# The order of TensorE's work in the last round of a mixture of experts: both halves of the down products ahead of the spread

## The chip, the cores and the metric

The kernel runs on one core of one Trainium2 chip. The metric is the device time of one launch in microseconds (us), the median over runs. TensorE (PE in the profile) multiplies, VectorE (DVE) and ScalarE (ACT) move and transform what it leaves in PSUM, GpSimd (POOL) fetches rows by index, SyncE (SP) issues the loads of the weights.

## The reference

One inference step of a two-layer decoder for 256 prompt tokens and 8 sample tokens (264 columns in the kernel), model width 1024. The first layer mixes tokens by retention, the second by gated linear attention (GLA); behind each mixer stands a mixture of 64 experts, of which each token takes 8. Cut to what matters here:

```
for i in range(2):
    h = modulate(x, norm_mix_g[i], sh1, sc1)
    x = x + g1 * mixer_i(h)                      # i = 0: retention, i = 1: GLA
    h = modulate(x, norm_ffn_g[i], sh2, sc2)     # RMS norm, scale, shift
    x = x + g2 * moe_ffn(h)
return rmsnorm(x, final_norm_g), states
# an expert on its rows: (silu(x @ w_gate) * (x @ w_up)) @ w_down,
#     w_gate, w_up: 1024 x 256, w_down: 256 x 1024, all float32, 1 MB each
# routed = sum over a token's 8 experts of weight * expert(row), and a shared expert is added
```

## The kernel before, in words

`experts(k, layer)` is called once for each layer. It goes through the 64 experts in 16 rounds of 4 (`ROUNDS`, `EPI`); rounds 13 to 15 are light ones, with 32 rows for each of the four experts, so that one tile of 128 rows holds the four. `LAST` is round 15. The weights pass through a ring of 12 slots of 1 MB: four gates, four ups, four downs of a round, issued by SP in that order (L2319 to L2359). In the last round the four down matrices come in two column halves: first the four first halves (semaphore `s_first_half`), then the four second halves (the slots' own semaphores, which `wait_light(pe, LAST, "moe_w_down")` waits for).

A light round on TensorE (`pe_round`, L2529): the gate products (`four_up`, L2449), then the spread of the round before (`spread`, L2510), which adds its rows to their tokens by a one-hot product for each of the 8 chunks of 128 model columns, then the up products (`four_up` again), two transposes of the hidden rows (`hidden_first`, L2526), a copy of them by ScalarE (L3016), and the down products (`four_down`, L2459): half 0 writes PSUM bank 6, half 1 bank 7, each 16 instructions over 512 columns. In the last round `pe_round` ends with half 0.

`last_spread` (L2481) follows. TensorE takes its instructions in order. It waits for ScalarE's copy of half 0 (`s_part`, L3038), multiplies chunks 0 to 3 (L2495, float32, two instructions each), then waits for the second halves of the down matrices and multiplies half 1, then chunks 4 to 7. Each chunk has PSUM bank 0 or 1 by turns, so that a chunk waits for VectorE's add of the chunk two before it (`s_add`; `add_last`, L2868 to L2873, three instructions, into x). `follow(pe, c)` is one step of what comes next and needs that add of chunk c: in layer 0 the sum of the squares of x over the chunk for the next norm (`nxt.sum`, L549, which waits for ScalarE's square, L532), in layer 1 three transposes of x for the output (`x_rows`, L1960). Before the change follow 0 and 1 stand behind half 1, and follow c - 2 behind each chunk c from 4 on; the caller (`tail_tensor`) issues follow 6 and 7.

ScalarE in the last round copies half 0 (L3038), then runs `beside_copies`: a small Sqrt that loads a table (L3403), and in layer 0 the squares of chunks 0 to 3; then it copies half 1, and in layer 0 squares chunks 4 to 7.

Behind layer 0's last sum come TensorE's conditioning products (L484), VectorE's norm (L566 to L575), ScalarE's shift (L543, eight chunks of h), and the first projection of GLA (L1403), which needs h and the first weights `in_gla_w_in`. Behind layer 1's last transposes come the output norm and the stores.

`keep_clock(k, bank, n)` (L470) issues n products of the identity with itself, 128x128 in float32, into a PSUM bank that nobody reads; one product is two instructions.

Of the kernel before, what the change touches and what calls it, by code (L numbers as in the profile page):

```python
# [21 lines left out]
P = 128  # L22
D = 1024
DC = D // P
TP = 256
NS = 8
T = TP + NS
# [35 lines left out]
LIGHT_BLOCKS = [(e, 32 * e) for e in range(EPI)]  # L63
# [217 lines left out]
LIGHT_PLACE = {ne: i for i, ne in enumerate(LIGHT_ROUND)}  # L281
# [5 lines left out]
def slot(k, n, inner):  # L287

    s = n % RING
    return k.ring[:, s * SLOT:(s + 1) * SLOT].rearrange("p (k n) -> p k n", n=inner)  # L290
# [179 lines left out]
def keep_clock(k, bank, products):  # L470

    for _ in range(products):
        k.nc.tensor.matmul(k.ps[:, bank, 0:P], k.ident, k.ident, start=True, stop=True)
# [22 lines left out]
def next_rows(k):  # L496

    return k.rstd[:, T:T + 256]
# [19 lines left out]
class Norm:  # L518
# [27 lines left out]
    def sum(self, pe, c):  # L546

        pe.wait_ge(self.s_sq, c + 1)
        mm = self.k.nc.tensor.matmul(self.sums_at, self.k.ones, self.sq[:, c, :], start=(c == 0), stop=(c == DC - 1))  # L549
        if c == DC - 1:  # L550
            mm.then_inc(self.s_sum, 1)
# [1494 lines left out]
def experts(k, layer):  # L2046

    nc, inp = k.nc, k.inp
# [14 lines left out]
    LAST = ROUNDS - 1  # L2063
    RANKED = NE - EPI

    def tiles(r):
        if not isinstance(r, int) or r < HEAVY:
            return PAIRS
        return PAIRS + 1 if r == HEAVY else 1

    def light(r):
        return tiles(r) == 1

    def done_tiles(r, late):
        return sum(tiles(q) for q in range(r)) if isinstance(r, int) else PAIRS * r + late
# [14 lines left out]
    last_token = slot_area[:, 0:T]  # L2090
# [19 lines left out]
    last_rows = row_area[:, 0:D]  # L2110
# [116 lines left out]
    def hidden_chunk(p, m):  # L2227
        return hid[:, p, :].rearrange("p (q m) -> p m q", m=FC)[:, m, :]

    def place(kind, e, of=PLACE):  # L2230
        return n_moe + of[(kind, e)]
# [222 lines left out]
    def four_down(p, blocks, half, of=PLACE):  # L2454

        for m in range(FC):
            for e, lo in blocks:
                n = place("moe_w_down", e, of)
                mm = nc.tensor.matmul(k.ps[lo:lo + 32, 6 + half, :], hid_t[:, p, m, lo:lo + 32],  # L2459
                                      slot(k, n, D)[:, m, half * 512:(half + 1) * 512],  # L2460
                                      start=(m == 0), stop=(m == FC - 1))
                if m == FC - 1 and half == 1 and blocks is HEAVY_BLOCKS and e == len(HEAVY_TILE) - 1:
                    mm.then_inc(h_done, 1)
                elif m == FC - 1 and half == 1 and (e, lo + 32) not in blocks:
                    mm.then_inc(k.ring_free[n % RING], 1)
        if half == 0:
            mm.then_inc(s_dn, 1)

    def wait_light(pe, r, name):

        for e in range(EPI):
            n = place(name, e, LIGHT_PLACE)
            pe.wait_ge(k.ring_full[n % RING], 16 * (r + n // RING + 1))
# [7 lines left out]
    def last_spread(pe, follow):  # L2481

        d = done_tiles(LAST, 0)
        pe.wait_ge(s_htc, LAST + 1)
        for half in range(2):
            if half:
                wait_light(pe, LAST, "moe_w_down")
                four_down(0, LIGHT_BLOCKS, 1, LIGHT_PLACE)
                if follow:
                    follow(pe, 0)  # L2490
                    follow(pe, 1)
            pe.wait_ge(s_part, 2 * d + 1 + half)
            for c in range(4 * half, 4 * half + 4):
                pe.wait_ge(s_add, DC * (LAST + 1) + c - 1)
                nc.tensor.matmul(k.ps[:, c % 2, 0:T], last_rows[:, c * P:(c + 1) * P], last_token,  # L2495
                                 start=True, stop=True).then_inc(s_scat, 1)
                if half and follow:
                    follow(pe, c - 2)

    def spread(pe, r, late=0, n=PAIRS):  # L2500

# [20 lines left out]
    def hidden_first(pe, p, bank, d, at=0):  # L2522

        pe.wait_ge(s_hid, d + p + 1)
        for m in range(FC):
            mm = nc.tensor.transpose(k.ps[:, bank, at + m * P:at + (m + 1) * P], hidden_chunk(p, m), ident)  # L2526
        mm.then_inc(s_hidt, 1)

    def pe_round(pe, r, late=0):  # L2529
        first, last = isinstance(r, int) and r == 0, isinstance(r, int) and r == LAST  # L2530
        heavy = tiles(r) > PAIRS
        d = done_tiles(r, late)
# [6 lines left out]
        for p in range(0 if light(r) or heavy else PAIRS):  # L2539
# [3 lines left out]
            for j, name in enumerate(("moe_w_gate", "moe_w_up")):  # L2543
# [3 lines left out]
                for c in range(DC):  # L2547
                    for e in (2 * p, 2 * p + 1):
                        n, lo = place(name, e), CAP * (e % 2)
                        w = slot(k, n, DE)  # L2550
                        if first and (name, e) in ROUND[0:EARLY]:
# [3 lines left out]
                                              start=(c == 0), stop=(c == DC - 1))  # L2555
                        if c == DC - 1:
                            mm.then_inc(k.ring_free[n % RING], 1)
        for j, name in enumerate(("moe_w_gate", "moe_w_up") if heavy else ()):
            for p in range(PAIRS):
# [3 lines left out]
                for c in range(DC):  # L2563
                    for e in (2 * p, 2 * p + 1):
# [3 lines left out]
                                              start=(c == 0), stop=(c == DC - 1))  # L2568
# [12 lines left out]
        for p in range(min(tiles(r), PAIRS)):  # L2581
            if heavy:
                hidden_first(pe, p, 6, d, at=p * DE)
            else:
                hidden_first(pe, p, 6 + p, d)
        if not last:
            if not first:
                pe.wait_ge(s_add, DC * r + DC)
            if not heavy:
                gather(pe, r + 1, late)  # L2590
            pe.wait_ge(s_htc, r + 1)
            if heavy:
                four_slots_first(pe, r).then_inc(h_done, 1)
            elif isinstance(r, int) and light(r + 1):
                four_slots_first(pe, r + 1).then_inc(s_ht, 1)
            else:
                slots_first(pe)
# [797 lines left out]
    def squares_of(act, chunks):  # L3395

        for c in chunks:
            act.wait_ge(s_add, DC * (LAST + 1) + c + 1)
            nxt.square(act, c)

    def beside_copies(act):

        nc.scalar.activation(silu[0:1, 0, 0:1], ident[0:1, 0:1], ACT.Sqrt)  # L3403
        if layer == 0:
            squares_of(act, range(DC // 2))

    def tail_scalar(act):

        rounds_scalar(act)
        act.wait_ge(s_cleared, 1)  # L3410
        pairs = extra_pairs["act"]
        here, more, usual, done = branch(act, "act", pairs, twice=True)
        with nc.body(more, valid_engines=here):
            scalar_round(act, LAST)
            with act.Fori(0, pairs) as i:
                for b in range(2):
                    act.wait_ge(x_gat, 2 * i + b + 1)
                    nc.scalar.copy(xg[:, 0, 4 * b:4 * b + 4, :].rearrange("p c n -> p (c n)"), k.ps[:, b, :])\
                        .then_inc(x_got, 1)
                act.wait_ge(x_own, i + 1)  # L3420
                act.wait_ge(x_scat, DC * i + DC)
                nc.scalar.copy(slot_token[:, 0, 0:TP].rearrange("p (t n) -> p t n", t=2),
                               k.ps[:, 4, 0:2 * EW].rearrange("p (t n) -> p t n", t=2)[:, :, 0:P])
                nc.scalar.copy(slot_token[:, 0, TP:T], k.ps[:, 4, TT * EW - 6 - NS:TT * EW - 6])\
                    .then_inc(x_tok, 1)
                act.wait_ge(x_gu, i + 1)
                nc.scalar.activation(silu[:, 0, :], k.ps[:, 2, 0:DE], ACT.Silu).then_inc(x_sil, 1)
                act.wait_ge(x_hidt, i + 1)
                nc.scalar.copy(hid_t[:, 0].rearrange("p m s -> p (m s)"), k.ps[:, 3, 0:DE]).then_inc(x_hidtc, 1)
                for half in range(2):  # L3430
                    act.wait_ge(x_dn, 2 * i + half + 1)
                    nc.scalar.copy(row_parts[:, 0, 0, half * 512:(half + 1) * 512], k.ps[:, 6 + half, :])\
                        .then_inc(x_hi, 1)
            nc.scalar.activation(silu[0:1, 0, 0:1], ident[0:1, 0:1], ACT.Sqrt)
            if layer == 0:
                act.wait_ge(x_add, pairs * DC + DC)
                for c in range(DC):
                    nxt.square(act, c)
            act.br(done)
        with nc.body(usual, valid_engines=here):  # L3440
            scalar_round(act, LAST, beside=beside_copies)
            if layer == 0:
                squares_of(act, range(DC // 2, DC))
            act.br(done)
        nc.switch_bb(done)
        if layer == 0:
            nxt.scalar(act)
            wait_used(k, act, next_group[-1])
            nc.scalar.copy(next_rows(k), k.ps[:, 4, 0:256]).then_inc(tail.s_rows, 1)
        else:  # L3450
            act.wait_ge(s_final, 1)
            final_squares(k, 0, sums, junk).then_inc(tail.s_sums, 1)
            act.wait_ge(s_final, 2)
            nc.scalar.activation(small, k.x[:, :, TP:T], ACT.Square).then_inc(s_final, 1)
            final_squares(k, 1, sums, junk).then_inc(tail.s_sums, 1)
# [34 lines left out]
```

## Time and profile before

| what | us |
|---|---|
| median of 3 runs | 1581.24 |
| lowest and highest | 1580.17, 1581.70 |
| the profiled execution, its own time | 1583.97 |
| the profiled execution, its span | 1582.1 |
| PE busy | 1492.0 |
| DVE busy | 701.7 |
| ACT busy | 358.4 |
| mean rate of the loads and stores | 367 GB/s |

### The profile page before, as it was taken

The page shows a single profiled execution, that of the slowest core. Times are in us where ns is not written, and L with a number is a line of the kernel's source. Part 1 is how long each engine was busy: PE and PEld are TensorE (multiplying, and loading weights), DVE is VectorE, ACT ScalarE, POOL GpSimd, SP SyncE. Part 2 cuts the span into 40 slices and gives each one's busy share as a digit, 9 for nine tenths or more (in the row PEclk, how much of TensorE's full clock was granted, in tenths as well). Part 3 has the DMA queues.
Part 4 walks back from the last instruction along what each step waited for, and adds up shares of the span by engine and source line. Part 5 has one row for each costly group of instructions (what it writes and reads, how often), then busy time and mean ns, then how long its engine had stood idle before and what let it go on. Part 6 is the DMA issues. An engine that isn't in the chain of part 4 may idle for free. (4 is left out here: it accounts for less than half of the span.)

```text
span 1582.1 us, 29469 instructions
## 1 busy us (share of the span) xinstructions
PE 1492.0 (94%) x11156; PEld 983.7 (62%) x11156; DVE 701.7 (44%) x1998; ACT 358.4 (23%) x760; POOL 92.0 (6%) x117
## 2 busy tenths in 40 slices
PE   6999999999999999999996899999999999999966
PEld 4778765687665566566553587776566566565533
DVE  3204535315465545534354335443745544543543
ACT  3012443203212111111120255432112211211111
POOL 0000100001000100000000000001000000010000
PEclk9999999999999999999998999999999999999988
DMA  9997699429999999999999983999999999999996
GB/s 363 389 369 270 252 399 399 184 101 370 392 412 420 420 420 420 421 418 419 413 384 415 358 280 120 347 364 335 416 419 421 420 420 420 420 419 414 391 407 247
DMA packets 153295, 580.27 MB, mean 367 GB/s; under 512 B 16893, under 2 KB 62113, under 8 KB 104938
## 3 DMA queue, kind: packets, MB, share of 16 engines
q1 hardware_dynamic: 137642, 535.74, 85.7%
q0 software_dynamic: 14912, 40.91, 6.7%
q10 hardware_dynamic: 640, 2.26, 0.4%
q8 instruction: 64, 1.05, 0.3%
q14 instruction: 37, 0.30, 0.1%
HBM read 566.12 MB, written 26.90 MB: 375 GB/s over the span
## 5 line engine op out<-in xcount | busy, mean ns | idle before, releaser
L2553 PE MATMUL ps<-ring,scratch 128*64 128x256 f32 x3008 | 330.7, 380 | 1.9 <-DMA ring<-in_moe_w_up 1.9
L2553 PEld LDWEIGHTS ps<-ring,scratch 128*64 128x64 f32 x3008 | 215.5, 137 | 107.2 <-issue 3.6
L2612 PE MATMUL ps<-ring,scratch 128*64 128x512 f32 x816 | 186.8, 598 | 1.2 <-DVE scratch L2970 0.9
L722 PE MATMUL ps<-hT,ring 128*128 128x264 f32 x768 | 179.4, 387 | 0.0
L2510 PE MATMUL ps<-scratch 128*128 128x264 bf16 x1344 | 165.9, 276 | 3.7 <-DVE xT L2873 2.0
L722 PEld LDWEIGHTS ps<-hT,ring 128*128 128x128 f32 x768 | 145.4, 191 | 28.9 <-issue 2.5
L2898 DVE SCALAR_TENSOR_TENSOR scratch<-scratch,ps 128x256 f32<-128x256 f32 x60 | 28.8, 481 | 302.2 <-ACT scratch L3007 280.2
L2510 PEld LDWEIGHTS ps<-scratch 128*128 128x128 bf16 x1344 | 116.7, 97 | 53.8 <-issue 15.4
L2865 DVE TENSOR_TENSOR scratch<-scratch,ps 128x264 f32<-128x264 f32 x224 | 95.3, 429 | 65.0 <-PE ps L2510 64.9
L2612 PEld LDWEIGHTS ps<-ring,scratch 128*64 128x64 f32 x816 | 53.3, 136 | 107.1 <-issue 75.1
L3007 ACT ACTIVATE scratch<-ps 128x256 f32<-128x256 f32 x60 | 23.1, 384 | 392.9 <-PE ps L2553 320.3
L2257 POOL DMA_INDIRECT scratch<-h_rows,scratch x58 | 57.7, 996 | 868.6 <-DVE scratch L2251 820.0
L3042 ACT CAST scratch<-ps 128x512 bf16<-128x512 f32 x112 | 65.5, 587 | 142.5 <-PE ps L2612 126.0
L2970 DVE TENSOR_TENSOR scratch<-ps,scratch 128x512 f32<-128x512 f32 x112 | 76.8, 686 | 34.5 <-ACT scratch L3042 34.5
L1403 PE MATMUL ps<-hT,ring 128*128 128x264 f32 x384 | 88.9, 386 | 1.9 <-DMA ring<-in_gla_w_in 1.9
L1403 PEld LDWEIGHTS ps<-hT,ring 128*128 128x128 f32 x384 | 72.0, 190 | 15.0 <-DMA ring<-in_gla_w_in 2.4
L2958 DVE TENSOR_TENSOR scratch<-scratch 128x512 bf16<-128x512 f32 x112 | 77.5, 692 | 3.9
L2416 PE MATMUL ps<-tab,scratch 128*128 128x128 f32 x464 | 62.8, 278 | 11.7 <-DVE scratch L2773 9.0
L2449 PE MATMUL ps<-ring,scratch 128*32 128x256 f32 x768 | 51.0, 424 | 19.5 <-DMA ring<-in_moe_w_gate 11.2
L2416 PEld LDWEIGHTS ps<-tab,scratch 128*128 128x128 f32 x464 | 50.2, 141 | 23.8 <-DVE scratch L2773 15.2
L2773 DVE COPY scratch<-ps 128x512 f32<-128x512 f32 x58 | 40.1, 692 | 56.0 <-PE ps L2416 56.0
L982 DVE SCALAR_TENSOR_TENSOR ring<-ring,rstd 128x512 f32<-128x512 f32 x64 | 41.3, 688 | 49.2 <-ACT rstd L1135 26.1
(413 smaller groups left out, 1542.3 us busy)
## 6 DMA issues: line engine op xcount, KB each, us to landing
ring<-in_moe_w_up SPq DMA_DIRECT2D x128, 1024.0 KB, 18.7
ring<-in_moe_w_gate SPq DMA_DIRECT2D x124, 1024.0 KB, 18.3
ring<-in_moe_w_down SPq DMA_DIRECT2D x118, 1024.0 KB, 15.9
ring<-in_ada_w SPq DMA_DIRECT2D x48, 1024.0 KB, 12.4
ring<-in_ret_w_in SPq DMA_DIRECT2D x24, 1024.0 KB, 16.8
ring<-in_state_ret SPq DMA_DIRECT2D x16, 1024.0 KB, 14.2
out_ret_sample<-ring POOLq DMA_DIRECT2D x16, 1024.0 KB, 8.9
ring<-in_gla_w_in SPq DMA_DIRECT2D x12, 1024.0 KB, 11.8
```

The lines of the kernel that those rows point to most:

```text
L722: mm = nc.tensor.matmul(k.ps[:, bank, 0:T], w[:, c, m * P:(m + 1) * P], k.h[:, c, :], start=(c == 0), stop=(c == DC - 1))
L1403: mm = nc.tensor.matmul(k.ps[:, bank, 0:T], w[:, c, m * P:(m + 1) * P], k.h[:, c, :], start=(c == 0), stop=(c == DC - 1))
L2257: pool.indirect_dma_start(xtok_of(p), None, h_rows[:, :], bass.IndirectOffsetOnAxis(ap=rows[:, p:p + 1], axis=0), bounds_check=ABSENT - 1, ...
L2416: mm = nc.tensor.transpose(k.ps[:, b, c * P:(c + 1) * P], xtok_of(p)[:, d0:d0 + P], ident)
L2449: mm = nc.tensor.matmul(k.ps[lo:lo + 32, bank, j * DE:(j + 1) * DE], xg_of(p)[:, c, lo:lo + 32], slot(k, n, DE)[:, c, :], start=(c == 0), ...
L2510: mm = nc.tensor.matmul(k.ps[:, c % 2, 0:T], parts_of(p)[:, s, c * P:(c + 1) * P], slot_token[:, p, :], start=(p == 0 and s == 0), stop=(p ...
L2553: mm = nc.tensor.matmul(k.ps[lo:lo + CAP, 2 + p, j * DE:(j + 1) * DE], xg[:, p, c, lo:lo + CAP], w[:, c, :], start=(c == 0), stop=(c == DC ...
L2612: mm = nc.tensor.matmul(k.ps[lo:lo + CAP, 6 + half, :], hid_t[:, p, m, lo:lo + CAP], w[:, m, half * 512:(half + 1) * 512], start=(m == 0), ...
L2865: nc.vector.tensor_tensor(acc[:, c, :], acc[:, c, :], k.ps[:, c % 2, 0:T], ALU.add).then_inc(s_add, 1)
L2958: nc.vector.tensor_tensor(parts_of(p)[:, 2, cols], rest[:, half], parts_of(p)[:, 1, cols], ALU.subtract).then_inc(s_part, 1)
L2970: nc.vector.tensor_tensor(rest[:, half], k.ps[:, 6 + half, :], parts_of(p)[:, 0, cols], ALU.subtract).then_inc(s_rest, 1)
L3042: nc.scalar.copy(parts_of(p)[:, 0, cols], k.ps[:, 6 + half, :]).then_inc(s_rhi, 1)
```

## The change

`last_spread` now runs half 1 of the down products directly behind half 0 (behind the wait for its weights), and only then all eight chunks of the spread; from chunk 2 on each chunk c is followed by follow c - 2. The waits of a chunk stay. In the second layer's last round, three `keep_clock` products stand ahead of the transposes of the hidden rows and six behind them, into bank 7. ScalarE no longer squares chunks 0 to 3 between its two copies in layer 0; it squares all eight behind the second copy.

```diff
     def last_spread(pe, follow):
 
         d = done_tiles(LAST, 0)
+
+        def second_half():
+            wait_light(pe, LAST, "moe_w_down")
+            four_down(0, LIGHT_BLOCKS, 1, LIGHT_PLACE)
+
+        def chunk(c):
+            pe.wait_ge(s_add, DC * (LAST + 1) + c - 1)
+            nc.tensor.matmul(k.ps[:, c % 2, 0:T], last_rows[:, c * P:(c + 1) * P], last_token,
+                             start=True, stop=True).then_inc(s_scat, 1)
+
         pe.wait_ge(s_htc, LAST + 1)
-        for half in range(2):
-            if half:
-                wait_light(pe, LAST, "moe_w_down")
-                four_down(0, LIGHT_BLOCKS, 1, LIGHT_PLACE)
-                if follow:
-                    follow(pe, 0)
-                    follow(pe, 1)
-            pe.wait_ge(s_part, 2 * d + 1 + half)
-            for c in range(4 * half, 4 * half + 4):
-                pe.wait_ge(s_add, DC * (LAST + 1) + c - 1)
-                nc.tensor.matmul(k.ps[:, c % 2, 0:T], last_rows[:, c * P:(c + 1) * P], last_token,
-                                 start=True, stop=True).then_inc(s_scat, 1)
-                if half and follow:
-                    follow(pe, c - 2)
+        second_half()
+        for c in range(DC):
+            if c % 4 == 0:
+                pe.wait_ge(s_part, 2 * d + 1 + c // 4)
+            chunk(c)
+            if follow and c >= 2:
+                follow(pe, c - 2)
 
@@ pe_round @@
             else:
+                if last and layer == 1:
+                    keep_clock(k, 7, 3)
                 hidden_first(pe, p, 6 + p, d)
+                if last and layer == 1:
+                    keep_clock(k, 7, 6)
@@ beside_copies, tail_scalar @@
         nc.scalar.activation(silu[0:1, 0, 0:1], ident[0:1, 0:1], ACT.Sqrt)
-        if layer == 0:
-            squares_of(act, range(DC // 2))
...
             scalar_round(act, LAST, beside=beside_copies)
             if layer == 0:
-                squares_of(act, range(DC // 2, DC))
+                squares_of(act, range(DC))
```

## Rows read from the trace of the kernel before

**Rows 1.** The page: span, busy time of PE.

```profile
span 1582.1 us, 29469 instructions
...
PE 1492.0 (94%) x11156; PEld 983.7 (62%) x11156; DVE 701.7 (44%) x1998; ACT 358.4 (23%) x760; POOL 92.0 (6%) x117
```

**Rows 2.** The chain that ended last, from 1515 us on: start, length, what.

```profile
1540.59 18.80 DMA ring<-in_moe_w_down
```

**Rows 3.** Timeline, end of layer 0: start, length, engine, line, operation, idle before.

```profile
873.28 1.92 PE L2459 MATMUL ps<-ring,scratch 128*32 128x512 f32 x16 [0.56 <-DMA ring<-in_moe_w_down]
...
875.95 1.13 PE L2495 MATMUL ps<-scratch 128*128 128x264 f32 x4 [0.74 <-issue]
...
877.35 1.25 PE L2495 MATMUL ps<-scratch 128*128 128x264 f32 x4 [0.28 <-DVE xT L2873]
...
878.96 1.92 PE L2459 MATMUL ps<-ring,scratch 128*32 128x512 f32 x16 [0.35 <-DMA ring<-in_moe_w_down]
...
880.81 1.16 PE L549 MATMUL ps<-scratch,tab 128*128 128x264 f32 x4
...
883.59 0.61 PE L2495 MATMUL ps<-scratch 128*128 128x264 f32 x2
...
884.48 0.61 PE L2495 MATMUL ps<-scratch 128*128 128x264 f32 x2
...
890.95 3.30 ACT L543 ACTIVATE hT<-hT,mod 128x256 f32<-128x256 f32 x8 [3.05 <-DVE hT L575]
...
892.47 7.39 PE L1403 MATMUL ps<-hT,ring 128*128 128x264 f32 x32 [1.89 <-DMA ring<-in_gla_w_in]
```

**Rows 4.** Timeline, end of layer 1.

```profile
1557.67 0.50 PE L2526 MATMUL ps<-tab,scratch 128*128 128x128 f32 x2 [0.65 <-DVE scratch L2898]
...
1559.53 3.55 PE L2459 MATMUL ps<-ring,scratch 128*32 128x512 f32 x16 [1.36 <-DMA ring<-in_moe_w_down]
...
1563.81 1.13 PE L2495 MATMUL ps<-scratch 128*128 128x264 f32 x4 [0.73 <-issue]
...
1566.41 1.92 PE L2459 MATMUL ps<-ring,scratch 128*32 128x512 f32 x16
...
1570.77 0.61 PE L2495 MATMUL ps<-scratch 128*128 128x264 f32 x2
...
1571.54 0.61 PE L2495 MATMUL ps<-scratch 128*128 128x264 f32 x2
```

**Rows 5.** Line L2359, SP's last two down loads: issue (first, last), time to landing.

```profile
L2359 SPq DMA_DIRECT2D ring<-in_moe_w_down x2: 997/1052/1107, 1551.6 to 1552.7; - x2
...
DMA to landing us min/median/max: 11.9/11.9/12.0
```

**Rows 6.** Timeline, TensorE's products behind idle time, both layers.

```profile
836.52 5.09 PE L2449 MATMUL ps<-ring,scratch 128*32 128x256 f32 x64 [2.60 <-DMA ring<-in_moe_w_up]
...
846.79 5.06 PE L2459 MATMUL ps<-ring,scratch 128*32 128x512 f32 x32 [2.94 <-DMA ring<-in_moe_w_down]
...
856.71 5.23 PE L2449 MATMUL ps<-ring,scratch 128*32 128x256 f32 x64 [4.86 <-DMA ring<-in_moe_w_gate]
...
1523.26 6.45 PE L2449 MATMUL ps<-ring,scratch 128*32 128x256 f32 x64 [3.09 <-DMA ring<-in_moe_w_up]
...
1533.48 3.64 PE L2459 MATMUL ps<-ring,scratch 128*32 128x512 f32 x32 [1.53 <-DMA ring<-in_moe_w_down]
...
1543.42 4.92 PE L2449 MATMUL ps<-ring,scratch 128*32 128x256 f32 x64 [6.30 <-DMA ring<-in_moe_w_gate]
...
1553.35 3.66 PE L2449 MATMUL ps<-ring,scratch 128*32 128x256 f32 x64 [0.17 <-DMA ring<-in_moe_w_up]
```

**Rows 7.** Stretches: busy time of each engine, then PEclk, DMA share, GB/s.

```profile
846.80:849.60 2.80, 2.80 (x16) 0.86 (x20) 0.00 (x0) 0.00 (x0) 0.00 (x0) 0.50 1.01 421
...
892.50:1095.00 202.50, 199.00 (x1191) 155.29 (x1193) 84.64 (x301) 79.24 (x174) 13.59 (x22) 1.00 0.82 288
```

**Rows 8.** Timeline, `keep_clock` products of the first mixer, eight of them.

```profile
241.28 2.05 PE L473 MATMUL ps<-tab 128*128 128x128 f32 x16
```

## The prediction

> **What bounds the kernel now.** I read the page first: TensorE is busy in 1492 of 1582 us [rows 1], so an instruction moved on TensorE counts wherever nothing covers it. Then the chain of waits at the end: the long piece is the load of the last down matrices, until 1559.4 [rows 2]. Near each layer's end TensorE waits for weights, and its order of work decides what is done inside those waits. Then the timeline of both ends [rows 3, 4].
>
> In layer 0 half 0 runs at 873.28 to 875.20, chunks 0 to 3 from 875.95 on, and half 1 at 878.96; it stood idle 0.35 us ahead of half 1 for its load [rows 3]. So the second halves land at about 878.9, and chunks 0 to 3 lie wholly in a wait that is there anyway. In layer 1 the last second half is issued at 1552.7 and takes 11.9 us [rows 5]: it lands at 1564.6. Half 0 took 3.55 us there in place of 1.92, the chunks began at 1563.81, and half 1 at 1566.41 [rows 4], 1.8 us after its load was there.
>
> **The move of half 1, layer 0.** The wait for the load now stands ahead of all eight chunks; behind it on TensorE's queue are the chunks, and for these wait VectorE's adds and ScalarE's squares. Half 1 can't start before 878.96, as before. It takes 1.85 us until the next instruction (878.96 to 880.81). Then chunk 0; its copy is long made. Chunks 0 and 1 have a bank each, and chunk 2 follows 1.40 us after chunk 0, since it waits for VectorE's add (875.95 to 877.35). From there the pattern is a chunk and a sum, 0.89 us each (883.59 to 884.48), of which there are five up to chunk 7: 880.81 + 1.40 + 5 x 0.89 = 886.66, against 884.48 before. Chunk 7 is 2.2 us later, and what follows it (sums 5 to 7, the norm's root, the scaling of h) keeps its length [rows 3]. ScalarE's move costs nothing of its own: chunk 0's add now ends after the copy of half 1 could, and one square (about 0.4 us) a chunk fits into 0.89.
>
> What covers some of it: GLA's first projection starts at 892.47, when its weights land, while ScalarE has the first chunk of h ready after an eighth of 3.30 us plus its latency, at about 891.4 [rows 3]. So 1.0 us of the 2.2 us is hidden, and 1.2 us goes to GLA's start. The conditioning products (3.7 us) stand ahead of it but end before h is ready. From 892.5 to 1095 TensorE is busy in 199.0 of 202.5 us, and DMA engines have room (share 0.82) [rows 7]; no wait there can take the delay up, and the slots of the ring come free later by as much. I carry it in full to the end; at best all of it is lost again in waits for loads behind 1500 us.
>
> **The move, layer 1.** Half 1 starts when the load is there, 1564.7 with 0.1 us of lag, rather than at 1566.41. Next instruction 1566.55, chunk 2 at 1567.95, then five steps of a chunk and three transposes at 0.78 us (1570.77 to 1571.54, 0.77 to 0.78): chunk 7 at 1571.85, against 1571.54 [rows 3, 4]. That is +0.3 us: the 1.8 us that half 1 wins are less than four chunks that no longer lie inside the wait. The tail behind chunk 7 keeps its length.
>
> **The small products.** Eight took 2.05 us, 0.26 each [rows 8]. Three take 0.77 us where TensorE stands idle 0.65 us for the hidden rows, six take 1.5 us where it stands idle 1.36 us [rows 4]. The first may delay the transposes by 0.1 us; the copy behind them ends some 0.9 us ahead of half 0's load, which covers that. The six may push half 0 by 0.2 us. None of it is on the path now, since half 1 waits for its load until 1564.6 whenever half 0 ends: cost 0, bound 0.2. What they can give is half 0 at clock 1.00, as in layer 0, 1.6 us shorter; but that gain ends in the wait for the second halves.
>
> **The clock in the new wait.** The reorder makes one idle stretch of TensorE in each layer: 875.2 to 878.96 in layer 0, 3.8 us, and in layer 1, with half 0 at full clock, 1559.6 + 1.9 = 1561.5 to 1564.7, 3.2 us. Rows 6 show what products do behind idle time. After 2.60, 2.94, 4.86, 3.09 and 6.30 us of it, groups that otherwise need 3.66 us (64 x 256 columns) or 3.64 us (32 x 512) took 5.09, 5.06, 5.23, 6.45 and 4.92: 1.4, 1.4, 1.6, 2.8 and 1.3 us more, at a granted clock of 0.50, which is 1.2 GHz [rows 6, 7]. After 1.53 us the group took its 3.64. No idle stretch from 2.6 us on in these rounds is without that loss. So I take 1.4 us, the commonest, for each of the two halves 1 and what follows it; bounds 0 and 2.8.
>
> The page "TensorE: Matmul & The Clock Gate" of the Trainium skill (Part 1, "HAM oscillation") speaks against the change in the same sense: short compute with a DMA wait behind it starts the next piece cold, and it advises to order the work so that the engine doesn't wait between. By that rule both halves 1 start at 1.2 GHz, which is the sum below; if it did not hold here the sum would be 1.5 us. The same part says that the activity window is free-running, so that the same kernel shows the fall at other places from run to run. The trace leaves that open: layer 0's half 0 took 1.92 us behind 0.56 us of idle time, layer 1's 3.55 behind 1.36 [rows 3, 4].
>
> **The sum.** Layer 0: 1.2 + 1.4. Layer 1: 0.3 + 1.4. Together +4.3 us. Against the profiled execution's own time, 1583.97, that is 1588.3; it lies 2.73 us above the median, so the median becomes 1581.24 + 4.3 = 1585.5. What a measurement of this kernel can tell from no change is about 0.2%, 3.2 us; 4.3 is a little over it.
>
> **The rivals.**
> A. The clock falls in one layer only, or the small products don't do what they should. If half 0 of layer 1 stays at 0.50 until 1563.1, only 1.6 us of idle time is left, and after 1.53 us nothing was lost [rows 6]: layer 1 costs 0.3. Sum 1.2 + 1.4 + 0.3 = +2.9, 1584.1. Against it: the products fill both gaps with work.
> B. The clock doesn't fall in either. +1.5, 1582.7. Against it: five of five.
> C. Layer 0's delay is taken up before the end, because loads set the pace of the last rounds (idle 3.09, 1.53 and 6.30 us for weights there [rows 6]). Then only layer 1 is left: +1.7, 1582.9. Against it: the loads wait for slots that TensorE frees, and it is 98% busy in GLA.
> D. Faster: without the profiler the second halves land earlier, so that there is no wait between the halves. It decides from a landing 1.2 us earlier in layer 0 (2.2 less the 1.0 hidden) and 0.3 us earlier in layer 1. If the load were there at half 0's end in both, layer 0: from 875.2 to chunk 7 takes 1.85 + 1.40 + 4.45 = 7.7 us, where it took 9.3, a gain of 1.6 as far as GLA's weights are earlier too; layer 1: the same 7.2 us (3.90 for the five steps) from half 0's end, which the small products bring to 1561.5: chunk 7 at 1568.7, a gain of 2.8. Sum -2.8 to -4.4 us, 1576.8 at best. Against it: the load streams without a break until then (18.8 us on the chain [rows 2]), and 12 us after issue is a queue, not a latency.
> E. The long fall (2.8 us) in one or both layers: +5.7 to +7.1, 1586.9 to 1588.3. One of five.
>
> **How the numbers follow.** Main case 0.42, A 0.22, B 0.09, C 0.13, D 0.06, E 0.08. The main case's own spread is 1 us to each side. Slower by more than 0.2% (over 1584.4): the main case but for a little, E, and some of A: 0.56. Same: most of A, B, C and the rest: 0.38. Faster: D, 0.06. Range: from 1582.0, which leaves out D and the weakest of C and B, to 1588.2, which leaves out E's upper part.
>
> **What would show it.** In the profile after: the DMA as what ends TensorE's idle time ahead of half 1 in both layers, 3 to 4 us long; half 1 (16 instructions) with more than 3 us in place of 1.92; four chunks in layer 0 no longer between the halves; GLA's first projection waiting for ScalarE's h rather than for weights, 2 to 3 us later than 892.5; half 0 of layer 1 at 1.92. The prediction is wrong if half 1 starts with no wait (D), if PEclk stays 1.00 across it (B), or if GLA's start doesn't move, which would mean that the weights land later than I read. If GLA's start moves and the ups of the last round start when they did before, C holds.

## The result, and the profile after

| | median, us | runs | against before |
|---|---|---|---|
| before | 1581.24 | 5 | |
| changed | 1588.70 | 5 | 1.0044 [1.0033, 1.0055], +7.0 us (5.2 to 8.7) |

The change makes the kernel slower, by 0.44%. In the experiments below one run of e1 (2096.91 us) and one run of the kernel before, beside e9 and e10 (3223.58 us), ran at a granted clock of 0.70 and 0.47 and are left out of the ratios. The profiled execution of the changed kernel took 1589.82 us, 5.85 more than that of before (1583.97).

The timeline of TensorE at the end of layer 0 in the changed kernel, the rows that answer to [rows 3] (chunks are now L2491):

```profile
872.33 1.93 PE L2459 MATMUL ps<-ring,scratch 128*32 128x512 f32 x16 [0.54 <-ACT scratch L3023]
877.87 3.64 PE L2459 MATMUL ps<-ring,scratch 128*32 128x512 f32 x16 [3.62 <-DMA ring<-in_moe_w_down]
881.44 2.69 PE L2491 MATMUL ps<-scratch 128*128 128x264 f32 x6
883.97 0.62 PE L549 MATMUL ps<-scratch,tab 128*128 128x264 f32 x2
884.42 0.61 PE L2491 MATMUL ps<-scratch 128*128 128x264 f32 x2
...
887.98 0.61 PE L2491 MATMUL ps<-scratch 128*128 128x264 f32 x2
...
895.11 7.36 PE L1403 MATMUL ps<-hT,ring 128*128 128x264 f32 x32 [1.04 <-ACT hT L543]
```

Between the halves TensorE now stands idle for 3.62 us, and the load ends that. Half 1 takes 3.64 us in place of 1.92. What ends the wait ahead of GLA's first projection is ScalarE's h, no longer the weights. From half 1's start to that projection it is 17.24 us, where it was 13.51 [rows 3]: 3.7 us more. The second load came 1.1 us earlier in this execution (877.87 against 878.96, with the same code ahead of it), so the projection is 2.64 us later.

The same at the end of layer 1, the rows that answer to [rows 4] (hidden rows L2529):

```profile
1547.91 5.85 PE L2449 MATMUL ps<-ring,scratch 128*32 128x256 f32 x64 [4.58 <-DMA ring<-in_moe_w_gate]
...
1558.53 3.66 PE L2449 MATMUL ps<-ring,scratch 128*32 128x256 f32 x64
1562.12 0.94 PE L473 MATMUL ps<-tab 128*128 128x128 f32 x6
1562.89 0.48 PE L2529 MATMUL ps<-tab,scratch 128*128 128x128 f32 x2
1563.21 1.50 PE L473 MATMUL ps<-tab 128*128 128x128 f32 x12
1564.64 1.92 PE L2459 MATMUL ps<-ring,scratch 128*32 128x512 f32 x16
1568.55 2.80 PE L2459 MATMUL ps<-ring,scratch 128*32 128x512 f32 x16 [1.99 <-DMA ring<-in_moe_w_down]
1571.28 2.69 PE L2491 MATMUL ps<-scratch 128*128 128x264 f32 x6
1573.80 0.49 PE L1960 MATMUL ps<-tab,xT 128*128 128x128 f32 x3
...
1577.23 0.61 PE L2491 MATMUL ps<-scratch 128*128 128x264 f32 x2
```

The small products fill both gaps, half 0 runs at 1.92 us, and then TensorE waits 1.99 us for the second load, not the 3 to 4 us that the prediction gave as a sign. From half 1's start to chunk 7 it takes 8.68 us.

Stretches of the changed kernel, columns as in [rows 7]: the wait and half 1 in layer 0, then two parts of its chunks; half 1 and the first chunks in layer 1.

```profile
874.30:877.80 3.50, 0.00 (x0) 0.00 (x0) 0.00 (x0) 2.07 (x3) 0.00 (x0) 0.82 0.88 275
877.90:881.40 3.50, 3.50 (x16) 0.62 (x16) 0.00 (x0) 0.00 (x0) 0.00 (x0) 0.50 1.02 408
881.50:883.90 2.40, 2.40 (x8) 1.45 (x7) 0.95 (x5) 1.01 (x2) 0.00 (x0) 0.61 1.02 415
884.00:888.40 4.40, 4.40 (x21) 3.67 (x21) 3.32 (x17) 2.12 (x5) 0.00 (x0) 1.00 1.05 382
...
1568.60:1569.80 1.20, 1.20 (x12) 0.47 (x16) 0.00 (x0) 0.14 (x1) 0.00 (x0) 0.86 0.33 133
1569.80:1573.70 3.90, 3.86 (x14) 1.60 (x7) 1.08 (x5) 0.58 (x1) 0.00 (x0) 0.61 0.01 4
```

In layer 0 the granted clock falls inside the wait (0.82 over it); all of half 1 runs at 0.50 (1.2 GHz), and the first three chunks for the most part too. In layer 1 the fall comes later and is divided between half 1 and the first chunks.

Of the 5.85 us between the two profiled executions, 2.6 are there at GLA's start and 1.9 more come in rounds of layer 1 whose code the change doesn't touch (last section). At the last round's gate products it is 4.5 us (1547.91 against 1543.42 [rows 6]), at its ups 5.2 (1558.53 against 1553.35), since the gates took 5.85 us in place of 4.92. Only 0.5 us come behind the ups, where layer 1's part of the change lies; the next section shows that the execution of before was slow there.

### The profile page after: what moved, and what is told of

It reads as the page before. It is cut to its first block and busy times, and to the rows that moved or that the text cites. A ratio compares the mean times of both kernels' runs of the same rounds, so it can differ in the third digit from the quotient of the medians.

```text
span 1588.0 us, 29505 instructions
## 1 busy us (share of the span) xinstructions
PE 1497.7 (94%) x11174; PEld 989.4 (62%) x11174; DVE 701.9 (44%) x1998; ACT 358.0 (23%) x760; POOL 91.9 (6%) x117
## 6 DMA issues: line engine op xcount, KB each, us to landing
ring<-in_ret_w_in SPq DMA_DIRECT2D x24, 1024.0 KB, 17.1
```

## The experiments

In each, the time is the ratio of the run's times to those of the kernel before on the same chip, with its 95% interval, turned into us.

**The small products alone** (e1): the kernel before with them.

```diff
+                if last and layer == 1:
+                    keep_clock(k, 7, 3)
                 hidden_first(pe, p, 6 + p, d)
+                if last and layer == 1:
+                    keep_clock(k, 7, 6)
```

> The kernel before with the nine small products in layer 1's last round, and the old order of the halves and chunks. Theory 1 (the chunks lose the cover of the wait for the down load, and the longer wait lets the clock fall): here the products are pure gain. Half 0 of layer 1 takes 1.92 us in place of 3.55, chunks 0 to 3 end 1.6 us earlier, half 1 starts when its load is there instead of 1.8 us later: 1.6 us less than before, about 1579.6. Theory 2 (the products themselves cost, by delaying the halves or by making the wait longer): 0 to +1 us. Theory 3 (the 7 us of the changed kernel come from the loads of the second layer's earlier rounds and have nothing to do with the order): no difference.

Measured: 1.0005 [0.9994, 1.0017], +0.8 us (-0.9 to +2.7). There is no gain of 1.6. Its timeline at half 0 of layer 1, and the same place in the next run but one (e3, layer 1 as before, no products):

```profile
1551.77 3.66 PE L2449 MATMUL ps<-ring,scratch 128*32 128x256 f32 x64 [1.04 <-DMA ring<-in_moe_w_up]
...
1557.86 1.92 PE L2459 MATMUL ps<-ring,scratch 128*32 128x512 f32 x16
...
1570.48 0.55 PE L1976 MATMUL ps<-tab,scratch 128*8 128x1 f32 x16 [0.34 <-ACT scratch L3458]
```

```profile
1559.95 3.66 PE L2449 MATMUL ps<-ring,scratch 128*32 128x256 f32 x64
1564.26 0.50 PE L2538 MATMUL ps<-tab,scratch 128*128 128x128 f32 x2 [0.65 <-DVE scratch L2910]
1565.36 1.92 PE L2459 MATMUL ps<-ring,scratch 128*32 128x512 f32 x16 [0.60 <-DMA ring<-in_moe_w_down]
...
1577.99 0.54 PE L1976 MATMUL ps<-tab,scratch 128*8 128x1 f32 x16 [0.35 <-ACT scratch L3464]
```

From the last ups to the last products over the sample rows (L1976) it takes 18.7 us with the small products and 18.0 without; in the profile of before it was 20.4 (1553.35 to 1573.77). Of these 2.4 us 1.6 are half 0 at 3.55 us, and 0.8 its load, which came 6.2 us behind the start of the ups instead of 5.4 [rows 4]. e8, the third execution of this code, took 18.0 too. So one of three was slow there, by chance as far as is known, and it is the one that the prediction started from. Where the clock holds by itself, the products push half 0 by 0.7 us (6.1 us behind the ups instead of 5.4), since its load is there by then.

**The order alone** (e2): the changed kernel without the products.

```diff
-                if last and layer == 1:
-                    keep_clock(k, 7, 3)
                 hidden_first(pe, p, 6 + p, d)
-                if last and layer == 1:
-                    keep_clock(k, 7, 6)
```

> The changed kernel without its nine small products. Theory 1: layer 0 as in the changed kernel, +3.7 us at the start of GLA against a fixed landing of the down load. In layer 1 half 0 at clock 0.50 ends about 1.6 us ahead of its second load; if the clock then holds, only +0.3 us there. Sum +4 us, about 1585.3, some 1.5 to 3 us under the changed kernel. Theory 2: the same sign, with all of layer 1's loss gone, up to 4 us under the changed kernel. Theory 3: as the changed kernel.

Measured: 1.0039 [1.0024, 1.0053], +6.2 us (3.8 to 8.4). The order carries the loss; the products add nothing that can be told (+7.0 with them, and +5.1 in the repeat below). In layer 0 its timeline is that of the changed kernel (3.64 us idle, half 1 at 3.64, 17.24 us to GLA's projection). In layer 1 it is not: the clock held across the wait. The ups of the round before the last and half 1:

```profile
1526.74 3.66 PE L2449 MATMUL ps<-ring,scratch 128*32 128x256 f32 x64 [2.85 <-DMA ring<-in_moe_w_up]
...
1567.53 1.92 PE L2459 MATMUL ps<-ring,scratch 128*32 128x512 f32 x16 [2.38 <-DMA ring<-in_moe_w_down]
```

From half 1 to chunk 7 it took 7.27 us here, against 8.68 in the changed kernel's first profile. Idle stretches of 2.38 and of 2.85 us were followed by products at full length, while one of 1.99 us was followed by slow ones.

**The new order in layer 0 only** (e3), with ScalarE's squares moved there; and **in layer 1 only** (e4), with the products.

```diff
+        if layer == 0:    # e4: layer == 1
+            wait_light(pe, LAST, "moe_w_down")
+            four_down(0, LIGHT_BLOCKS, 1, LIGHT_PLACE)
+            for c in range(DC):
...
+            return
         for half in range(2):
```

> The new order in layer 0 alone, ScalarE's squares moved there with it, layer 1 as before, no small products. Theory 1: half 1 of layer 0 over 3 us long, GLA's first projection waits for h, 2.6 to 3.7 us later than its weights, and this is carried to the end: +2.6 to +3.7 us, 1584 to 1585. If the last rounds of layer 1 take up a delay from upstream, +0 to +1. Theory 3: what it shows in layer 1's heavy rounds is the same in this run and in the kernel before.

> The new order in layer 1 alone, with the nine small products, layer 0 as before. Theory 1: the load of the second halves sets half 1's start; from its landing to chunk 7 8.7 us as in the changed kernel against 6.9 before: +1.8 us, about 1583.0. Theory 3: no difference.

Measured: e3 1.0018 [1.0004, 1.0033], +2.8 us (0.6 to 5.2); e4 1.0018 [1.0005, 1.0030], +2.8 us (0.8 to 4.7). In e3, half 1 and GLA's first projection:

```profile
880.16 3.43 PE L2459 MATMUL ps<-ring,scratch 128*32 128x512 f32 x16 [3.60 <-DMA ring<-in_moe_w_down]
...
896.79 3.58 PE L1403 MATMUL ps<-hT,ring 128*128 128x264 f32 x15 [1.04 <-ACT hT L543]
```

16.6 us from the one to the other, 3.1 more than before. In e4, the end of layer 1 from the last ups:

```profile
1553.85 3.66 PE L2449 MATMUL ps<-ring,scratch 128*32 128x256 f32 x64 [0.97 <-DMA ring<-in_moe_w_up]
...
1564.54 3.29 PE L2459 MATMUL ps<-ring,scratch 128*32 128x512 f32 x16 [2.67 <-DMA ring<-in_moe_w_down]
...
1575.40 0.55 PE L1976 MATMUL ps<-tab,scratch 128*8 128x1 f32 x16 [0.35 <-ACT scratch L3470]
```

21.6 us, against 18.0 to 18.7 in the executions of the old order whose half 0 ran at 1.92. This is the slowest of four executions of the new order: e2 took 19.1 and the repeat below 19.6, both with half 1 at 1.92. The two layers' parts add up to 5.6.

**The clock held in the new wait** (e5): the changed kernel with products between the halves.

```diff
         def second_half():
+            keep_clock(k, 7, 7 if layer else 12)
             wait_light(pe, LAST, "moe_w_down")
```

> The changed kernel with more small products between half 0 and the wait for the second load: 12 in layer 0 (2.9 us of a wait of 3.6), 7 in layer 1 (1.8 us of 2.0 to 2.7). Theory 1a (a part of the loss is the clock that falls in the new wait): half 1 takes 1.92 us in both layers, chunk 2 follows chunk 0 after 1.4 us; from half 1 to chunk 7 in layer 0 7.7 us in place of 10.1. 2.4 us less than the changed kernel from layer 0 and about 1 from layer 1: about +3.5 us against the kernel before, where only the lost cover is left. Rival 1b (the clock costs nothing that counts, all is the lost cover): as the changed kernel, +7.

Measured: 1.0024 [1.0013, 1.0036], +3.8 us (2.1 to 5.7). Layer 0:

```profile
875.49 2.94 PE L473 MATMUL ps<-tab 128*128 128x128 f32 x24
878.96 1.92 PE L2459 MATMUL ps<-ring,scratch 128*32 128x512 f32 x16 [0.52 <-DMA ring<-in_moe_w_down]
880.82 1.16 PE L2492 MATMUL ps<-scratch 128*128 128x264 f32 x4
882.25 0.71 PE L2492 MATMUL ps<-scratch 128*128 128x264 f32 x2 [0.28 <-DVE xT L2881]
...
893.94 4.24 PE L1403 MATMUL ps<-hT,ring 128*128 128x264 f32 x18 [1.04 <-ACT hT L543]
```

Half 1 happens to start at 878.96, as before, and GLA's projection 15.0 us later, against 13.5 before and 17.2 in the changed kernel. So of layer 0's 3.7 us, 1.5 are the lost cover and 2.3 the clock. Rival 1b is out for that stage. In layer 1 half 1 took 1.92 us and 7.27 to chunk 7, as in e2, where the clock had held without products. In the whole time e5 stands 3.2 us under the first measurement of the changed kernel and 1.3 under the repeat.

**No wait between the halves** (e6, e7): most of the second load left out, in the old and in the new order, both with the nine products.

```diff
-            cols = slice(half * 512, (half + 1) * 512)
+            cols = slice(half * 512, half * 512 + (8 if half else 512))
```

> The kernel before with the nine small products, and of each second half of the last round's down matrices in both layers only 8 of 512 columns are loaded (the rest is left out, so the loads are 4 MB shorter in all). It serves only as the measure for the next kernel: no wait is left between the halves. Under the kernel before by what the chunk part waits less, mostly in layer 1: the loads behind come 5 us earlier. Some 1 to 6 us less.

> The changed kernel with the same loads left out (8 of 512 columns of the second halves). Theory 1 (what hurts in the new order is the wait for the second load that stands ahead of the chunks): with the load there, the new order is the faster one. From half 0's end to chunk 7 it takes 7.2 to 7.7 us against 8.5 to 9.3 in the old order: 1.6 us less in layer 0, 1.3 in layer 1, 2.9 us under the kernel of the old order with the same loads. Theory 4 (the new order itself is slower, wait or no wait, as it packs chunks and follow-ups more densely on VectorE and ScalarE): above it by 2 us or more.

Measured: e6 1.0005 [0.9994, 1.0016], +0.8 us; e7 0.9980 [0.9971, 0.9990], -3.2 us (-4.6 to -1.6). The medians of the two differ by 3.1 us, where theory 1 had 2.9. Half 0 and the projection in e6, then in e7:

```profile
871.58 1.92 PE L2459 MATMUL ps<-ring,scratch 128*32 128x512 f32 x16 [0.46 <-ACT scratch L3020]
...
889.49 7.36 PE L1403 MATMUL ps<-hT,ring 128*128 128x264 f32 x32 [1.03 <-ACT hT L543]
```

```profile
873.35 3.64 PE L2459 MATMUL ps<-ring,scratch 128*32 128x512 f32 x32 [0.46 <-ACT scratch L3023]
...
890.22 7.39 PE L1403 MATMUL ps<-hT,ring 128*128 128x264 f32 x32 [1.20 <-DMA ring<-in_gla_w_in]
```

This decides it: with the load there the new order is the faster one, and theory 4 falls. By stages it is 16.9 us from half 0 to the projection in place of 17.9, and 17.3 from layer 1's last ups to L1976 in place of 18.8: 2.5 of the 3.1 us. So what loses in the changed kernel hangs on the wait for the second load. And e6 isn't measurably faster than before (-0.9 to +2.5) although 4 MB fewer are loaded, where 1 to 6 us had been expected. In layer 1 it takes as long as e1 (18.8 and 18.7 us). In layer 0 it is 1.3 us shorter from half 0 to the projection (17.9 against 19.2), as neither half 1 nor the projection waits for a load there; the whole time doesn't show that. So the old order hides the second load wholly in layer 1, and in layer 0 perhaps not quite.

**ScalarE's squares alone** (e8): the kernel before with that part of the change.

```diff
-        if layer == 0:
-            squares_of(act, range(DC // 2))
...
-                squares_of(act, range(DC // 2, DC))
+                squares_of(act, range(DC))
```

> The kernel before with ScalarE's squares of chunks 0 to 3 moved behind its second copy, the order on TensorE as before. It costs that part of the change by itself: sums 0 and 1 wait for the squares, about 1.2 us in layer 0, of which 1.0 us is hidden ahead of GLA's weights: 0 to +0.5 us.

Measured: 1.0005 [0.9996, 1.0014], +0.8 us (-0.6 to +2.2). The first sum waited 1.08 us for its square:

```profile
881.66 1.16 PE L549 MATMUL ps<-scratch,tab 128*128 128x264 f32 x4 [1.08 <-ACT scratch L532]
```

And the projection started on h instead of on its weights, 13.8 us behind half 1 in place of 13.5. As expected, and small.

**Products in three more waits** (e9), a try for a better kernel in the old order, with the nine products in layer 1 too.

```diff
+        if last:
+            keep_clock(k, 5, 16)      # ahead of the last round's gate products
         if light(r):
             wait_light(pe, r, "moe_w_gate")
...
+            keep_clock(k, 5, 6)       # ahead of GLA's first projection
             for t in range(first_gate):
```

> The kernel before with the nine small products in layer 1, 16 more ahead of the last round's gate products in both layers (3.8 us in a wait of 3.8 to 6.3) and 6 ahead of GLA's first projection (1.5 us in a wait of 1.9), all in places where TensorE waits for loads; the order of halves and chunks is the old one. If a slow clock behind waits is worth saving where products are not gated by the next load: the gate products of the last round take 3.7 us in place of 4.9 to 6.5, GLA's first projection never 9.1 in place of 7.4, 1 to 2 us less, about 1580. If the loads set the pace there anyway: no difference.

Measured: 1.0017 [1.0008, 1.0027], +2.7 us (1.3 to 4.3). Slower, a miss. In layer 1 its 16 products started late and at the slow clock:

```profile
1541.35 5.44 PE L473 MATMUL ps<-tab 128*128 128x128 f32 x32 [4.26 <-issue]
1546.72 3.66 PE L2450 MATMUL ps<-ring,scratch 128*32 128x256 f32 x64
```

They ended at 1546.7, with the gate products directly behind them. In the profile of before these started at 1543.42 [rows 6]. In layer 0 they held the clock for the gates (3.66 us), but then TensorE waited 2.93 us for the ups and did those at 5.34 us. What TensorE waited for in the 4.26 us the profile doesn't show; how the 2.7 us divide stays open.

**The changed kernel again** (e10), unaltered.

> The changed kernel once more, unaltered, beside the kernel before on the same chip, to see whether the two parts (+2.8 and +2.8 us, layer 0 alone and layer 1 alone) add up to it: +5.6 us if they add, more than 7 if the parts make each other worse.

Measured: 1.0032 [1.0019, 1.0044], +5.1 us (3.0 to 7.0). Together with the first measurement, +7.0, this agrees with a plain sum of the two layers' parts, 5.6; intervals of 4 us leave room for more than that. Half 1 in layer 0, then in layer 1:

```profile
876.76 3.64 PE L2459 MATMUL ps<-ring,scratch 128*32 128x512 f32 x16 [3.57 <-DMA ring<-in_moe_w_down]
...
1567.35 1.92 PE L2459 MATMUL ps<-ring,scratch 128*32 128x512 f32 x16 [2.05 <-DMA ring<-in_moe_w_down]
```

With its loads intact no version beat the kernel before.

**All profiled executions with their loads intact, by stage** (us; "rounds" are the three of the last section):

| | order, layer 0 | half 1 to GLA's projection | rounds | order, layer 1 | last ups to L1976 |
|---|---|---|---|---|---|
| before | old | 13.5 | 91.1 | old | 20.4 |
| e8 | old, squares late | 13.8 | 91.1 | old | 18.0 |
| e1 | old | 13.8 | 91.1 | old, products | 18.7 |
| e9 | old, products | 13.0 | 91.7 | old, products | 18.7 |
| e4 | old | 13.5 | 91.1 | new, products | 21.6 |
| e3 | new | 16.6 | 91.3 | old | 18.0 |
| changed | new | 17.2 | 93.0 | new, products | 20.9 |
| e10 | new | 17.4 | 92.3 | new, products | 19.6 |
| e2 | new | 17.2 | 92.4 | new | 19.1 |
| e5 | new, products in wait | 15.0 | 92.5 | new, products in wait | 20.2 |

Without the products in the wait, the new order costs 3.5 us on average in layer 0 (17.1, against 13.6 in before, e1 and e4) and 1.5 in layer 1 (20.3 against 18.8, each spread over 2.4 us).

## Why the prediction was right, and where its sizes were off

- **The cover.** Right. The wait for the load now stands ahead of all chunks, half 1 starts no earlier, and the four chunks come behind it. e5 shows layer 0's part alone: 1.5 us where 1.2 were forecast.
- **The clock, layer 0.** Right as a mechanism, too small as a term. It was put at 1.4 us, the commonest excess in [rows 6], and was 2.3 (e5 against the changed kernel): half 1 took 1.7 us more, and from chunk 0 to chunk 3 it was 3.0 us, where e5 took 2.4. In [rows 7] the clock was at 0.50 for 2.8 us of a group's work; here it was at 0.50 for all 3.5 us of half 1 and for most of the next 2.4 (PEclk 0.61). The four executions with this wait and nothing in it (changed, e2, e3, e10) agree: 16.6 to 17.4 us to the projection.
- **The clock, layer 1.** Half right. The wait was put at 3.2 us and was 2.0 to 2.7. In two of four executions the clock fell, and from half 1 to chunk 7 it took 8.6 to 8.7 us, against 6.94 from the load's landing to chunk 7 before (1564.6 to 1571.54): +1.7, as forecast. In the other two (e2, e10) it held, and it was 7.27, the +0.3 of the order alone. So the 1.4 us are the size of the fall but not its average, and a fall in one layer only, rival A's outcome, is what e2 and e10 had.
- **"No idle stretch from 2.6 us on in these rounds is without that loss".** True of the five in the one profile, not in general: e2's ups followed 2.85 us of idle time at 3.66 us.
- **The base, layer 1.** Off by about 2 us. Before's 20.4 us were taken as this layer's usual end; the four other executions of the old order took 18.0 to 18.7. The prediction had noted, from the Trainium skill's page "TensorE: Matmul & The Clock Gate" (Part 1), that the fall moves from run to run, and left it open. The traces agree: half 0 of layer 1, the same instructions, took 3.55 us before and 1.92 in e3 and e8. A kernel that is slow by chance in the one profile is faster in the median than that profile says. That layer 1's 1.5 us by stages come near the forecast 1.7 is luck: a base too slow and a fall counted as certain cancel. e4's whole time, +2.8 (0.8 to 4.7), holds both.
- **Carrying through.** Right. The delay at the projection (2.64 us) is there at the row fetches behind it (2.6 us up to 1300 us), and nothing of it is taken up in the last rounds: it is 4.5 us at the last gates and 5.2 at the last ups. Rival C is out.
- **The rounds between.** A term that the sum left out. "I carry it in full to the end" counted no new wait on the way: the changed kernel lost another 1.2 and 1.9 us in rounds whose code is the same (e10 and its first profile; last section).
- **The small products.** "Cost 0, bound 0.2" holds in the new order, where half 1 waits anyway. In the old one they cost 0.7 us when half 0's load is early.
- **Rival D.** Not the case here, but its mechanism is real: e7 measured it, with the size that was worked out for it in the expectation.
- **The sum.** +4.3 us against +7.0 (5.2 to 8.7) and +5.1 (3.0 to 7.0). By the ratio the changed kernel stands at 1588.2, the very top of the range; its median, 1588.70, lies just above. The way and the cause were right, the size was at the edge. By stages the shortfall is about 1 us in layer 0 (3.5 for 2.6), most of it the clock, and about 1 us in the rounds.

## What to carry to other kernels

When an engine takes its work in order and must wait for a load, look at what it did in that wait before moving the wait forward: here four chunks lay in it and cost nothing, and packing the work more densely behind it could not win that back. A new idle stretch of TensorE has two prices, what no longer lies in it and the slow clock behind it, and the second was the larger one in layer 0. Before a change to an order is judged by one profile, compare that stage in several executions: a stage that ran slow by chance makes the change look cheaper than it is. To see whether a wait is what costs, take its load away in both orders, as e6 and e7 did: the order that lost by some 6 us won by 3.

## What the runs showed that was not expected

The rounds of layer 1 ahead of round 12 (two tiles of 128 rows each; the expectations call them heavy) run the same code in all kernels, at 30.37 us a round, but in some executions TensorE comes to wait for the up matrices, and three rounds lose some tenths to a whole microsecond each. GpSimd's first row fetch of such rounds (start, length, idle before), before and then changed, and one of the waits in the changed kernel:

```profile
1297.34 0.98 POOL L2257 DMA_INDIRECT scratch<-h_rows,scratch  x1 [28.08 <-DVE scratch L2251]
...
1388.43 0.99 POOL L2257 DMA_INDIRECT scratch<-h_rows,scratch  x1 [28.09 <-DVE scratch L2251]
```

```profile
1299.93 0.99 POOL L2257 DMA_INDIRECT scratch<-h_rows,scratch  x1 [28.06 <-DVE scratch L2251]
1330.52 0.98 POOL L2257 DMA_INDIRECT scratch<-h_rows,scratch  x1 [28.31 <-DVE scratch L2251]
1361.73 0.99 POOL L2257 DMA_INDIRECT scratch<-h_rows,scratch  x1 [28.93 <-DVE scratch L2251]
1392.95 0.99 POOL L2257 DMA_INDIRECT scratch<-h_rows,scratch  x1 [28.94 <-DVE scratch L2251]
```

```profile
1369.54 3.67 PE L2556 MATMUL ps<-ring,scratch 128*64 128x256 f32 x32 [0.67 <-DMA ring<-in_moe_w_up]
```

The three rounds took 91.09 us before and 93.02 in the changed kernel. Whether this belongs to the change stays open. Against it: e6, in the old order, lost 1.6 us there, and e7, in the new one, nothing. For it: with the loads intact the five executions with the new order in layer 0 lost 0.2 to 1.9 us (e3 the least), 1.2 on average, and the five with the old order nothing, but for 0.6 in e9. If it does belong to the change, it is the about 1 us that neither the clock nor the cover accounts for. What decides it was not tried.

Elsewhere too single executions of one kernel differ by several us: from GLA's first projection to the first row fetch behind it, e3, e4 and e8 took 1.2 to 1.9 us more than the others, and the 35 runs of before beside e5 to e8 went from 1578.7 to 1587.8. So a change of some 3 us needs many runs, and where it acts has to be read stage by stage.
